# In-projection weights from the sixth tile on: rounded part by a casting transfer, remainder by a transfer that adds onto the negated rounded part

## The reference, cut to what matters

```python
xn = rmsnorm(x, p['norm_mix_pre'])
proj = xn @ p['w_in']                        # the in-projection
q, k, v, o, ig, fg, u, gates = jnp.split(proj, SPLITS, axis=-1)
```

## Time and profile before

| | |
|---|---|
| median of three runs | 1964.41 us (1963.36 to 1967.33) |
| profiled execution, its own time | 1965.83 us |
| its span in the trace | 1964.1 us |
| granted TensorE clock, mean | 0.997 of full speed |
| PE busy | 1941.4 us (99%) |
| DVE busy | 1268.6 us (65%) |
| ACT busy | 775.4 us (39%) |
| POOL busy | 23.5 us (1%) |
| HBM read / written | 160.24 MB / 50.37 MB |

### The profile page before, as it was taken

How to read it: one execution, slowest core, us unless ns; L and a number is a source line. 1 busy time by engine, 2 the same in 40 slices (tenths; PEclk the granted TensorE clock), 3 DMA queues, 4 the chain that set the end, 5 groups by cost and what they waited for, 6 DMA issues and landing times.

```text
span 1964.1 us, 30693 instructions
## 1 busy us (share of the span) xinstructions
PE 1941.4 (99%) x12783; PEld 1917.9 (98%) x12783; DVE 1268.6 (65%) x1655; ACT 775.4 (39%) x1423; POOL 23.5 (1%) x59
## 2 busy tenths in 40 slices
PE   9999999999999999999999999999999999999997
PEld 8999999999999999999999999999999999899997
DVE  6896777776777754453445548977777777636363
ACT  5422222322323234463222335645445444535342
POOL 0000000000000000000000000000000000000000
PEclk9999999999999999999999999999999999999999
DMA  3221112212111334555531304122222222555654
GB/s 132 65 73 49 51 58 76 56 54 89 56 55 49 120 110 151 189 180 209 190 134 44 137 27 149 67 71 84 78 70 85 78 68 99 193 198 201 201 180 156
DMA packets 90138, 212.61 MB, mean 108 GB/s; under 512 B 15372, under 2 KB 50572, under 8 KB 90000
## 3 DMA queue, kind: packets, MB, share of 16 engines
q1 hardware_dynamic: 90000, 210.64, 32.4%
HBM read 160.24 MB, written 50.37 MB: 107 GB/s over the span
## 4 chain that ended last, share of the span: by engine, by line
PE 90%; DVE 6%; DMA 1%; issue 1%; ACT 1%; SPq 0%; POOL 0%; DVEq 0%; ACTq 0%; POOLq 0%
PE ps L854 17%; PE ps L856 17%; PE ps L855 17%; PE ps L1121 7%; PE ps L1122 7%; PE ps L1123 7%; PE ps L1155 4%; PE ps L1156 4%; PE ps L1157 4%; PE ps L925 2%; PE ps L922 1%; DVE cacc L1867 1%; PE ps L905 1%; PE ps L923 1%; PE ps L902 1%
## 5 line engine op out<-in xcount | busy, mean ns | idle before, releaser
L854 PE MATMUL ps<-rx,fhi 128*128 128x364 f32 (+2 forms) x1752 | 585.7, 334 | 0.6 <-DVE flo L1690 0.6
L856 PE MATMUL ps<-rx,flo 128*128 128x364 f32 (+2 forms) x1752 | 571.7, 326 | 0.0
L855 PE MATMUL ps<-rx,fhi 128*128 128x364 f32 (+2 forms) x1752 | 571.5, 326 | 0.0
L1867 DVE SCALAR_TENSOR_TENSOR cacc<-glub,pars,cacc 128x1118 f32<-128x1118 f32 x240 | 331.5, 1381 | 5.6
L854 PEld LDWEIGHTS ps<-rx,fhi 128*128 128x128 f32 x1752 | 329.6, 188 | 2.8 <-issue 1.3
L855 PEld LDWEIGHTS ps<-rx,fhi 128*128 128x128 f32 x1752 | 329.6, 188 | 1.5
L856 PEld LDWEIGHTS ps<-rx,flo 128*128 128x128 f32 x1752 | 329.3, 188 | 0.0
L1155 PE MATMUL ps<-ghi,dhi 128*128 128x384 f32 (+1 forms) x528 | 174.3, 330 | 3.7 <-DVE glo L2181 2.9
L1156 PE MATMUL ps<-glo,dhi 128*128 128x384 f32 (+1 forms) x528 | 173.3, 328 | 0.0
L1157 PE MATMUL ps<-ghi,dlo 128*128 128x384 f32 (+1 forms) x528 | 173.1, 328 | 0.0
L2174 DVE TENSOR_TENSOR dlo<-draw,dhi 128x1408 fp32r<-128x1408 f32 x48 | 77.7, 1624 | 120.5 <-ACT dhi L1575 120.5
(11 more groups left out here) (281 smaller groups left out, 3993.1 us busy)
## 6 DMA issues: line engine op xcount, KB each, us to landing
fraw<-wts SPq DMA_DIRECT2D x84, 512.0 KB, 3.7
draw<-wdn SPq DMA_DIRECT2D x48, 704.0 KB, 4.2
uraw<-wts SPq DMA_DIRECT2D x44, 512.0 KB, 4.4
scr_g<-cva SPq DMA_DIRECT2D x22, 512.0 KB, 2.6
graw<-scr_g SPq DMA_DIRECT2D x43, 192.0 KB, 4.2
fx<-x SPq DMA_DIRECT2D x8, 544.0 KB, 8.3
scr_ga<-spl SPq DMA_DIRECT2D x8, 544.0 KB, 5.0
scr_gb<-spl SPq DMA_DIRECT2D x8, 544.0 KB, 4.3
```

The lines of the kernel that those rows point to most:

```text
L854: pe.matmul(b, hi[:, w], src[:, his[k], cols], start=(k == 0), stop=False)
L855: pe.matmul(b, hi[:, w], src[:, los[k], cols], start=False, stop=False)
L856: mm = pe.matmul(b, lo[:, w], src[:, his[k], cols], start=False, stop=(k == KB - 1))
L1867: op = dve.scalar_tensor_tensor(a[:, :], g[:, j:j + AW], pars[:, at:at + 1], a[:, :], ALU.mult, ALU.add)
```

## The change

For the tiles 5 to 64 (`N_BY_DVE` = 5) the raw values no longer come to SBUF on their own:

- POOL issues `fhi <- wts`, a transfer whose destination has the format fp32r, so that it rounds on the way (`whole`). It does so when tile n-3 is finished, as SP did.
- ACT writes `flo` = -`fhi` (`minus`), at the place where it wrote `fhi` before.
- POOL waits for that and issues `flo <- wts` with accumulation (`rest`): `wts` is added onto what stands in `flo`, which gives the remainder.
- PE waits for this second transfer (`w_acc`) in place of DVE's `w_lo`.

SP no longer issues these 60 transfers (it keeps the wait on `grp_done` at the place), and DVE no longer subtracts for them. The tiles 0 to 4 and all from 65 on are made as before. Three semaphores are merged into others to make room, without a change in order, and counts of `w_lo` are shifted by `LO0` = 60.

```diff
+N_BY_DVE = 5
...
@@ SP @@
                 if is_last(s) and kind not in ("mu", "var"):
                     sp.wait_ge(grp_done, s + 1)
-                    weights(tile + 3)
+                    if tile + 3 < N_BY_DVE or tile + 3 >= N_IN:
+                        weights(tile + 3)
                     tile += 1
...
@@ POOL @@
-            for i in range(len(STEPS)):
-                p = i % 2
-                pool.wait_ge(dsm, 5 * i + 5)
-                pool.tensor_tensor(sm[p][:, 6:7], sm[p][:, 4:5], eps[:, 1:2], ALU.pow).then_inc(rs_set, 1)
+
+            def whole(n):
+                pool.dma_start(fhi[n % 3][:, :], wts[n]).then_inc(w_cast, 16)
+
+            def rest(n):
+                pool.wait_ge(w_hi, n + 1)
+                pool.dma_start(flo[n % 3][:, :], wts[n], accum_op=ALU.add).then_inc(w_acc[n % 2], 16)
+
+            tile = 0
+            for s in range(NS):
+                i = step_at(s, 1)
+                if i is not None:
+                    p = i % 2
+                    pool.wait_ge(dsm, 5 * i + 5)
+                    pool.tensor_tensor(sm[p][:, 6:7], sm[p][:, 4:5], eps[:, 1:2], ALU.pow).then_inc(rs_set, 1)
+                if is_last(s) and SLOTS[s][0][0] not in ("mu", "var"):
+                    tile += 1
+                    if N_BY_DVE <= tile + 1 < N_IN:
+                        rest(tile + 1)
+                    if N_BY_DVE <= tile + 2 < N_IN:
+                        pool.wait_ge(grp_done, s + 1)
+                        whole(tile + 2)
...
@@ PE @@
                     if c == 0:
-                        pe.wait_ge(w_lo, n + 1)
+                        if n < N_BY_DVE:
+                            pe.wait_ge(w_lo, n + 1)
+                        else:
+                            pe.wait_ge(w_acc[n % 2], ACC_IN[n])
...
@@ ACT @@
+            def minus(n):
+
+                act.wait_ge(w_cast, 16 * (n + 1 - N_BY_DVE))
+                act.activation(flo[n % 3][:, :], fhi[n % 3][:, :].bitcast(F32), ACT.Copy, scale=-1.0).then_inc(w_hi, 1)
...
-                    if n + 2 >= 3:
+                    if N_BY_DVE <= n + 2 < N_IN:
+                        minus(n + 2)
+                    elif n + 2 >= 3:
                         whole(n + 2)
...
@@ DVE @@
-                    if n + 2 >= 3:
+                    if 3 <= n + 2 < N_BY_DVE or n + 2 >= N_IN:
                         rest(n + 2)
```

More of the change, by code:

```diff
@@ L136 @@
 CONV0, CONV_SLOTS = 11, 18
+N_BY_DVE = 5
+BY_POOL = [sum(1 for i in range(N_BY_DVE, N_IN) if i % 3 == s) for s in range(3)]
+C_STORED = 32 * KB // 2
+LO0 = N_IN - N_BY_DVE
+ACC_IN = [16 * sum(1 for i in range(N_BY_DVE, n + 1) if i % 2 == n % 2) for n in range(N_IN)]
 N_GATE = IN_TILES.index(("gate", 0))
@@ L215 @@
 DH_W = FB // 2 * P
-W_DOWN = (16 * FB, 16 * (N_RING // 3))
+W_DOWN = (16 * FB, 16 * (N_RING // 3 - BY_POOL[0]))
 N_DN = N_STR + (FB - N_PLAIN) * len(PAIR)
@@ L445, in build @@
         w_lo = sem("w_lo")
+        w_cast = sem("w_cast")
+        w_acc = [sem(f"w_acc{s}") for s in range(2)]
         grp_done = sem("grp_done")
@@ L491, in build @@
         xc_set = sem("xc_set")
-        xc_out = [sem(f"xc_out{s}") for s in range(2)]
         csq_sq = sem("csq_sq")
@@ L551, in build @@
         y_half = sem("y_half")
-        ft_out = sem("ft_out")
         y_sto = [sem(f"y_sto{s}") for s in range(2)]
@@ L650, in _ @@
                     for j in range(2):
-                        sp.wait_ge(c_sto[j], 32 * KB // 2)
+                        sp.wait_ge(c_sto[j], C_STORED)
                         sp.dma_start(cs[j][:, :], scr_c[j]).then_inc(cs_in[j], 16)
@@ L655, in _ @@
                     sp.wait_ge(xc_set, j + 1)
-                    sp.dma_start(scr_xc[j], cs[j % 2][:, :]).then_inc(xc_out[j % 2], 16)
+                    sp.dma_start(scr_xc[j], cs[j % 2][:, :]).then_inc(c_sto[j % 2], 16)
                     if j + 2 < KB:
                         sp.wait_ge(csq_sq, j + 1)
-                        sp.wait_ge(xc_out[j % 2], 16 * (j // 2 + 1))
+                        sp.wait_ge(c_sto[j % 2], C_STORED + 16 * (j // 2 + 1))
                         sp.dma_start(cs[j % 2][:, :], scr_c[j + 2]).then_inc(cs_in[j % 2], 16)
@@ L662, in _ @@
                     for j in range(2):
-                        sp.wait_ge(xc_out[j], 16 * KB // 2)
+                        sp.wait_ge(c_sto[j], C_STORED + 16 * KB // 2)
                 for j in range(KB):
@@ L801, in _ @@
                     sp.wait_ge(ft_set, 2 * FB)
-                    sp.dma_start(ffn_tail, ftail[:, :]).then_inc(ft_out, 16)
+                    sp.dma_start(ffn_tail, ftail[:, :]).then_inc(m_sto, 16)
                 if c and m == 3:
@@ L808, in _ @@
             sp.wait_ge(y_sto[1], 32)
-            sp.wait_ge(ft_out, 16)
-            sp.wait_ge(m_sto, 16)
+            sp.wait_ge(m_sto, 32)
             for j in range(2):
@@ L993, in _ @@
             for n in range(KB):
-                pe.wait_ge(w_lo, PB0 + n + 1)
+                pe.wait_ge(w_lo, PB0 + n + 1 - LO0)
                 for c in range(NC):
@@ L1001, in _ @@
             for n in range(KB):
-                pe.wait_ge(w_lo, PA0 + n + 1)
+                pe.wait_ge(w_lo, PA0 + n + 1 - LO0)
                 for c in range(NC):
@@ L1033, in _ @@
                     if m not in seen:
-                        pe.wait_ge(w_lo, WO0 + m + 1)
+                        pe.wait_ge(w_lo, WO0 + m + 1 - LO0)
                 else:
@@ L1053, in _ @@
                     pe.wait_ge(plain_set, PLAIN_EVAC[q - 6])
-                pe.wait_ge(w_lo, lo_of(j, 1))
+                pe.wait_ge(w_lo, lo_of(j, 1) - LO0)
                 if (j, t) == (0, 0):
@@ L1111, in _ @@
                             pe.wait_ge(o_log, 8)
-                    pe.wait_ge(w_lo, lo_of(j, A_TURN[prod]))
+                    pe.wait_ge(w_lo, lo_of(j, A_TURN[prod]) - LO0)
                     if j == N_PLAIN and prod in (5, 6, 7, 4):
@@ L1150, in _ @@
                     if k % (FB // 2) == 0:
-                        pe.wait_ge(w_lo, N_WLO + 2 * n + k // (FB // 2) + 1)
+                        pe.wait_ge(w_lo, N_WLO + 2 * n + k // (FB // 2) + 1 - LO0)
                     if m == 0:
@@ L1169, in whole @@
             def whole(n):
-                act.wait_ge(w_in[n % 3], 16 * (n // 3 + 1))
+                act.wait_ge(w_in[n % 3], 16 * (n // 3 + 1 - (n >= N_IN) * BY_POOL[n % 3]))
                 act.activation(fhi[n % 3][:, :], fraw[n % 3][:, :], ACT.Copy).then_inc(w_hi, 1)
+            def minus(n):
+                act.wait_ge(w_cast, 16 * (n + 1 - N_BY_DVE))
+                act.activation(flo[n % 3][:, :], fhi[n % 3][:, :].bitcast(F32), ACT.Copy, scale=-1.0).then_inc(w_hi, 1)
             act.preload_act_table_set("natural_log_exp_and_others")
```

## The result

| | before | this kernel |
|---|---|---|
| median of 16 runs each | 1964.55 us (1963.36 to 1967.33) | 1968.66 us (1965.2 to 1972.07) |
| profiled execution, its own time | 1965.83 us | 1970.52 us |
| its span in the trace | 1964.1 us | 1968.3 us |
| granted TensorE clock, mean | 0.997 | 0.995 |

The account below looks back on a forecast made before the run. PE was taken as the bound, busy 1941.4 of 1964.1 us, with at most 2.9 us to win back. Terms 0 + 0 + 0 + 2 + 0.5 = +2.5 us gave 1968.3 profiled, 1966.9 median, range 1961.5 to 2010.

Parts of the forecast that it names:

- the forecast case: Whole kernel: no change to speak of, 1966.9 us, own range 1962 to 1968.3, chance 0.45.
- 0 (DVE) + 0 (SP, ACT): In-projection: 73 us of DVE subtractions and SP's 60 issues go, hidden; ACT's negation takes 1.05 us as before; 0 us.
- 0 (usual tiles): Usual weight tiles: the adding transfer lands after 5.3 us against 9.9 available, hidden with 4.6 us to spare; 0 us.
- every such tile late: Rival: adding transfer slow in itself, passing 9.9 us at 12 tiles; +45 us at its upper bound, 2010; chance 0.22.
- 2 (first pass): First pass, 782 to 810 us: two adding transfers delay the store and load chain PE waits on; +2 us.
- one excess of 1.6 us and a little of the second: First pass: how the 2 us was chosen for two adding transfers on the chain, between nothing and 6.4 us.
- Faster: Rival: the 2.3 us wait goes as SP's store no longer follows a plain load; at best -2.9 us, 1961.5; chance 0.06.
- 0.5 (second pass): Second pass, 856 to 866 us, transfer engines full: adding transfer issued at 860.2 lands 0.4 to 3.6 us late; +0.5 us.
- 6.1 us at one place: Tile ending at 809.43 us: 6.1 us left for the adding transfer, 5.3 taken, so hidden by 0.8 us.
- its price, nearer the lower row: Adding transfer's landing taken as 5.3 us, between a plain 512 KB load's 3.7 and a crowded 544 KB one's 11.6.
- a few us slower: Rival: crowded places cost upper bounds, 6.4 + 3.6 us, plus 0.9 at the tile ending at 809.43; +11 us, 1975; chance 0.27.
- The rule that the prediction weighed: POOL's issues: DVE in two-port mode locks out GpSimd's descriptor writing, making an issue up to 0.85 us late; sum unchanged.

Follow-up runs that it names:

- e5: The change with the first pass of the layer norm given one slot more at its end: 1965.98 us, ratio 1.0004.
- e7: The change for tiles 5 to 54 only, tiles 55 to 64 made the old way: 1964.68 us, ratio 1.0000.
- e4: The change with the second transfer a plain casting one that overwrites flo instead of adding: 1965.33 us, ratio 1.0006.
- e11: The kernel before with only tiles 55 to 64 by POOL's casting and adding transfers, and one slot more in the first pass: 1965.78 us, ratio 1.0008.
- e8: The kernel before with only tiles 55 to 64 by POOL's casting and adding transfers: 1965.47 us, ratio 1.0004.
- e2: The kernel before with only tiles 57 and 58 by POOL's casting and adding transfers: 1963.94 us, ratio 0.9995.
- e1: The change with tiles 57 and 58 made the old way: 1967.64 us, ratio 1.0011.
- e12: The change with POOL's adding transfer issued ahead of the step's power operation, without the extra slot: 1968.59 us, ratio 1.0024.

## Why the prediction was nearly right

The time was forecast at 1966.9 and is 1968.7, 0.4 us above the forecast case's own range (1962 to 1968.3) and well inside the whole one. DVE's time was hidden, the usual tiles were free and the first pass cost some 2 us of waiting, as forecast. The second pass cost nothing, two terms were missing, and how the 2 us came about was in part luck. By its own steps:

- **"0 (DVE) + 0 (SP, ACT)".** Right. DVE's subtractions are 73 us less and PE gains 0.4 us of the 0.6. ACT's negation takes 1.05 us, as taken. The page's DVE busy time is 1203 and not 1196, probably since neighbours overlap by 0.08 us at their ends, so that less busy time goes with each; the group itself has the 73.
- **"0 (usual tiles)".** Right, with less to spare than said. An adding transfer lands after 5.7 us (5.3 taken), and POOL's issue is 0.88 us where 0.5 was taken; in the trace the next one starts 0.6 us after it. The casting transfer lands 6.6 us after its own issue, 7.2 after the adding one's; the text had 402.7 - 394.8 = 7.9. ACT waited for it once, 0.4 us. The rival "every such tile late" needed 9.9 us. The longest landing of an adding transfer anywhere was 9.7 us, after 885 us, where PE didn't wait for it.
- **"2 (first pass)".** The wait grew by 1.9 us. The timelines show the late load behind it, e5 and e7 that the cost needs this chain's tightness and the crowded tiles, and e4 points at the adding. How the 2 was reached isn't right: "one excess of 1.6 us and a little of the second" was really 3.3 + 2.9 = 6.2 us, next to the 6.4 named as the most, and 4.0 us came back since SP's weight loads no longer stand ahead of two stores, a gain that the prediction named under the rival "Faster" and left out of the sum. Two errors of opposite sign made the net right, and that was luck.
- **"0.5 (second pass)".** 0. The adding transfers issued from 846 to 885 us land after 5.5 to 6.6 us, not 8.3 to 11.5: the windows around them are as full as in the earlier trace rows, but the adding transfers didn't suffer what the plain load issued at 856.13 did.
- **6.1 us at one place, "by 0.8 us" hidden.** In the change it landed after 6.1 us, at 808.8, and PE's first matmul of the tile starts at 809.62: 0.8 us of cover, as the text had it. But here the adding transfer had a start of 0.83 us on SP's load. With a start of 0.4 us or less it took 7.1 to 9.1 us (e11, e8, e5, e2), and PE waited 1.4 us in e5 and 0.3 in e8. The step "its price, nearer the lower row" was taken from calm places and used in a crowded one.
- **Missing: the clock.** The prediction priced a longer wait at its own length. In the profiled execution the wait brought half clock for 6.8 us and cost 2.6 us more than itself; over the runs this is some 1 us, an estimate.
- **Missing: 0.45 us outside the span.** The kernels with 58 or 60 pairs have 1.97 to 2.29 us there, those with none, 2, 10 or 50 have 1.78 to 1.82. That it steps between 50 and 58 pairs isn't explained, nor is it shown that the pairs themselves cause it.

The sum for a profiled execution was 1965.83 + 2.5 = 1968.3, and it took 1970.52. The 2.2 us between are 2.6 (clock) + 0.45 (outside) - 0.5 (second pass) - 0.4 (the `flo` waits at the start) - 0.1 (first pass) = 2.05. The interval of the ratio, +2.4 to +4.9 us, includes the bound of 0.2%, so "about no change, on the slower side" is what can be said. Of the rivals, "a few us slower" (+11 us) had a price nearly three times too high, and of its three places only the first pass cost anything in the change.

Adding issues take 854 to 913 ns at all 60 tiles, and DVE's later taps take 1382 ns in the mean against 1381 before. The casting issues take up to 0.89 us at 57 tiles and 1.18 us at three. These are the three that are under way when a first tap of DVE begins, at 292, 465 and 637 us (POOL's and DVE's timelines):

```profile
292.47 1.18 POOL L842 DMA_DIRECT2D fhi<-wts  x1
292.69 0.86 DVE L1897 TENSOR_SCALAR cacc<-glub,pars 128x1118 f32<-128x1118 f32 x1
```

POOL's issue ends 0.1 us after the tap, and the tap isn't longer than before. The rule that the prediction weighed (the Trainium skill, SBUF — State Buffer, Who interferes with whom: DVE's two-port modes lock out GpSimd's writing of descriptors) agrees with this trace. It costs 0.3 us at three of 120 issues, and PE waits for none of them. In e4 the casting issues at these three places take 0.54 us, as elsewhere.

**What stays open.** Why the runs of the change spread over 7 us (4 before), beyond the clock; a last load that lands after 4 or 7 us by a few tenths of a us would do it, and isn't shown over the runs. The same may be why e7 and e8 add up to 0.6 us and not 4.1: in the profiled executions the last load takes 4.2 us in e8 and 7.1 in the change. Where e11's 1.5 us lie and where e1 still loses 2.2 us is open too. The intervals of single kernels (1.8 us) don't reach further.

## What to carry to other kernels

A change that frees an engine for which PE waits 0.6 us in all can win little by that, so cost what replaces it: here the new transfers were free, to within 1.8 us, at 50 of 60 places and cost where a chain of stores and loads already bound the step. Before adding traffic to such a stretch give its chain a slot of room (some 2.9 us with the change). Another order in POOL's queue won nothing without that room (e12). A wait that hangs on which of two transfers goes out first by tenths of a us can't be priced from calm places. And a wait of PE that grows by 2 us may cost more than the 2: look at the granted clock behind it.

## What the runs showed of the hardware

- At the first pass's wait the granted clock stayed at 1.00 when PE stood for 2.3 or 2.5 us, was half for 3.4 us behind 3.7, and half for 6.8 us behind 4.2. With 4.0 us of matmuls ahead of a rest of 2.3 us it stayed up. The length of one wait doesn't settle it: near 1693 us a wait of 2.0 us brought 3.4 us of half clock in the kernel before and in the change, and none in e1.
- 512 KB from device memory to f32 in SBUF, issued by SP, lands after 3.7 us in the median; to fp32r, issued by POOL, after 4.3 (the first of e4's pairs); with adding, after 5.7. The casting transfer behind the adding one in POOL's queue lands after 6.6, behind a casting one after 5.2. That POOL's issue and the cast share in the 0.6 us between the first two wasn't taken apart.
- Two transfers of some 0.5 MB that go out together share the time unevenly: SP's load lands after 4.2 us and POOL's adding one after 7.1 to 7.6 where they go out within 0.2 us of each other (e8, e11), and after 7.1 and 6.1 where POOL's has a start of 0.8 us (the change).
- POOL is busy for 0.88 us with each of an adding pair's issues in the median, and for 0.54 to 0.57 where no transfer adds (e4). A casting issue that is under way when DVE's first tap (0.86 us) begins takes 1.18 us, at three places of the change. The issues of a pair start about 0.6 us apart in both.
- A run's time outside its span depends on the kernel: 1.8 us, and 2.3 with 60 pairs of transfers by POOL.
